# Two output tiles of a feed-forward chunk multiplied side by side, matmuls alternating between PSUM banks

## What is computed

```
def swiglu(x, w_gate, w_up, w_down):
    return (jax.nn.silu(x @ w_gate) * (x @ w_up)) @ w_down

f = swiglu(rms_norm_2(h, ffn1_norm_pre[l]), ffn1_w_gate[l], ffn1_w_up[l], ffn1_w_down[l])
h = h + 0.5 * rms_norm_2(f, ffn1_norm_post[l])
```

## Time and profile before

| what | value |
|---|---|
| median of 3 runs | 2175.87 us (2174.8 to 2176.27) |
| span of the profiled execution | 2173.0 us (its own time is not listed) |
| instructions | 24012 |
| PE busy | 92% |
| DVE, ACT busy | 53%, 37% |
| mean granted TensorE clock | 0.956 of full speed |
| transfers | 91 GB/s on average |

### The profile page before, as it was taken

How to read it: one execution, slowest core, us unless ns; L and a number is a source line. 1 busy time by engine, 2 the same in 40 slices (tenths; PEclk the granted TensorE clock), 3 DMA queues, 4 the chain that set the end, 5 groups by cost and what they waited for, 6 DMA issues and landing times.

```text
span 2173.0 us, 24012 instructions
## 1 busy us (share of the span) xinstructions
PE 2001.3 (92%) x8722; PEld 1578.5 (73%) x8722; DVE 1157.6 (53%) x1447; ACT 793.2 (37%) x971; POOL 43.3 (2%) x103
## 2 busy tenths in 40 slices
PE   4899999989999999799999997899996989999997
PEld 3687888866777777477888885676664757888885
DVE  4545666469354454455433456489744555433455
ACT  2326554233355544333222233223435243222232
POOL 2000000000000000000000000000000000000000
PEclk7899999989999999899999998999998989999997
DMA  8234556411222121023324322232211223324321
GB/s 309 91 113 140 182 160 178 145 58 59 77 59 59 39 59 39 20 78 97 92 87 111 97 73 82 77 98 78 57 41 39 78 58 97 92 87 111 97 73 63
DMA packets 293433, 198.28 MB, mean 91 GB/s; under 512 B 6690, under 2 KB 283508, under 8 KB 293364
## 3 DMA queue, kind: packets, MB, share of 16 engines
q1 hardware_dynamic: 284148, 163.79, 26.1%
q0 software_dynamic: 9216, 33.56, 4.6%
HBM read 195.21 MB, written 2.11 MB: 91 GB/s over the span
## 4 chain that ended last, share of the span: by engine, by line
PE 81%; DVE 10%; ACT 4%; issue 3%; SPq 1%; DMA 1%; DVEq 0%; ACTq 0%
PE acc L567 20%; PE acc L569 20%; PE acc L568 20%; PE acc L734 3%; PE acc L736 3%; PE acc L735 3%; PE ob L792 2%; PE sc L751 2%; DVE s_rstd L1416 1%; ACT s_w_high L1000 1%; PE acc L942 1%; PE ob L775 1%; DVE s_k_rt L1607 1%; PE acc L944 1%; PE acc L943 1%
## 5 line engine op out<-in xcount | busy, mean ns | idle before, releaser
L567 PE MATMUL acc<-s_h_high,s_w_high 128*128 128x512 f32 x1376 | 551.5, 401 | 38.2 <-DVE s_h_low L1389 16.9
L568 PE MATMUL acc<-s_h_low,s_w_high 128*128 128x512 f32 x1376 | 541.0, 393 | 0.0
L569 PE MATMUL acc<-s_h_high,s_w_low 128*128 128x512 f32 x1376 | 540.8, 393 | 0.0
L1378 DVE TENSOR_TENSOR s_w_low<-s_raw,s_w_high 128x2048 fp32r<-128x2048 f32 x160 | 366.7, 2292 | 301.9 <-ACT s_w_high L1000 301.4
L567 PEld LDWEIGHTS acc<-s_h_high,s_w_high 128*128 128x128 f32 x1376 | 261.5, 190 | 105.8 <-issue 41.6
L1000 ACT ACTIVATE s_w_high<-s_raw 128x2048 fp32r<-128x2048 f32 x160 | 305.0, 1906 | 9.9 <-DVE s_cols L1471 9.8
L569 PEld LDWEIGHTS acc<-s_h_high,s_w_low 128*128 128x128 f32 x1376 | 261.6, 190 | 55.4
L568 PEld LDWEIGHTS acc<-s_h_low,s_w_high 128*128 128x128 f32 x1376 | 262.1, 190 | 54.2 <-issue 2.2
L567 PE MATMUL acc<-s_b_high,s_w_high 128*128 128x512 f32 x640 | 257.2, 402 | 34.3 <-DVE s_branch L1920 16.4
L568 PE MATMUL acc<-s_b_low,s_w_high 128*128 128x512 f32 x640 | 252.8, 395 | 0.0
L569 PE MATMUL acc<-s_b_high,s_w_low 128*128 128x512 f32 x640 | 252.5, 395 | 0.0
(11 more groups left out here) (242 smaller groups left out, 2129.9 us busy)
## 6 DMA issues: line engine op xcount, KB each, us to landing
s_raw<-in_a_w_in SPq DMA_DIRECT2D x48, 512.0 KB, 5.0
s_raw<-in_ffn_w_gate SPq DMA_DIRECT2D x44, 512.0 KB, 3.9
s_raw<-in_ffn_w_up SPq DMA_DIRECT2D x44, 512.0 KB, 5.1
s_raw<-in_w_in SPq DMA_DIRECT2D x36, 512.0 KB, 4.3
s_raw<-in_b_w_in SPq DMA_DIRECT2D x32, 512.0 KB, 5.0
s_ada_w<-in_a_ada_w POOLq DMA_DIRECT2D x24, 512.0 KB, 6.5
s_ada_w<-in_b_ada_w POOLq DMA_DIRECT2D x24, 512.0 KB, 4.4
s_raw<-in_ffn_w_down SPq DMA_DIRECT2D x32, 384.0 KB, 3.9
```

Source lines behind the costliest of these rows:

```text
L567: pe.matmul(acc[b][:, :], w_high[:, o:o + P], hi, start=(k == 0), stop=False, skip_group_check=grouped)
L568: pe.matmul(acc[b][:, :], w_high[:, o:o + P], lo, start=False, stop=False, skip_group_check=grouped)
L569: mm = pe.matmul(acc[b][:, :], w_low[:, o:o + P], hi, start=False, stop=(k == nk - 1), skip_group_check=grouped)
L1378: dve.tensor_tensor(w_low[:, w], raw[:, w], w_high[:, w].bitcast(F32), ALU.subtract).then_inc(w_ready, 1)
```

## The change

PE makes the gate and the up tile of a chunk together. For each slice of k it issues six matmuls, gate and up in turn: high x high for both, high x low for both, low x high for both. The tiles go to `acc[0]`, `acc[1]` for chunks of slot 0 and to `sc[0]`, `sc[1]` for those of slot 1. Before a chunk PE waits for both counts, in the loops for one chunk less than before. In layer 1 the matmul of the sum of squares now stands behind all 48 matmuls of the first chunk; in layer 2 each of the eight stands behind six matmuls. DVE reads from the new banks; its order and ACT's are as they were.

```
+        gu_bank = [[acc[0], acc[1]], [sc[0], sc[1]]]
...
+            def both(tq, s, ready=None, base=0, between=None):
+
+                for t in range(2):
+                    pe.wait_ge(evac[t], tq)
+                for k in range(KD):
+                    if ready is not None:
+                        pe.wait_ge(ready, base + k + 1)
+                    hi, lo = h_high[:, k * T:(k + 1) * T], h_low[:, k * T:(k + 1) * T]
+                    o = [s * SLOT + paired(k, t) for t in range(2)]
+                    for t in range(2):
+                        pe.matmul(gu_bank[s][t][:, :], w_high[:, o[t]:o[t] + P], hi, start=(k == 0), stop=False,
+                                  skip_group_check=True)
+                    for t in range(2):
+                        pe.matmul(gu_bank[s][t][:, :], w_high[:, o[t]:o[t] + P], lo, start=False, stop=False,
+                                  skip_group_check=True)
+                    for t in range(2):
+                        mm = pe.matmul(gu_bank[s][t][:, :], w_low[:, o[t]:o[t] + P], hi, start=False,
+                                       stop=(k == KD - 1), skip_group_check=True)
+                        if k == KD - 1:
+                            mm.then_inc(tile_ready, 1)
+                    if between is not None:
+                        between(k)
...
                     for s in range(2):
                         chunk(q0 + s)
-                        for t in range(2):
-                            first = part == "a" and s == t == 0
-                            if first and l == 2:
-                                pe.wait_ge(ms_ready, 6)
-
-                            product(t, t0 + s, s, paired, t, h_high, h_low, 0, KD,
-                                    *((h_ready, hb) if first else ()),
-                                    between=(lambda k: sum_square(6, k)) if first and l == 2 else None)
-                            if first and l == 1:
-                                sums(2)
+                        first = part == "a" and s == 0
+                        if first and l == 2:
+                            pe.wait_ge(ms_ready, 6)
+
+                        both(t0, s, *((h_ready, hb) if first else ()),
+                             between=(lambda k: sum_square(6, k)) if first and l == 2 else None)
+                        if first and l == 1:
+                            sums(2)
                     with pe.Fori(1, nk // 2) as i:
                         for s in range(2):
                             chunk(2 * i + (q0 + s))
-                            for t in range(2):
-                                product(t, 2 * i + (t0 + s), s, paired, t, h_high, h_low, 0, KD)
+                            both(2 * i + (t0 + s - 1), s)
...
-                            dve.tensor_tensor(sg[s][:, :], rstd[:, :], acc[0][:, :], ALU.mult).then_inc(evac[0], 1)
+                            dve.tensor_tensor(sg[s][:, :], rstd[:, :], gu_bank[s][0][:, :], ALU.mult).then_inc(evac[0], 1)
                             dve.wait_ge(tile_ready, 2 * n + (t0 + 2))
-                            dve.tensor_tensor(hd[s][:, :], rstd[:, :], acc[1][:, :], ALU.mult).then_inc(evac[1], 1)
+                            dve.tensor_tensor(hd[s][:, :], rstd[:, :], gu_bank[s][1][:, :], ALU.mult).then_inc(evac[1], 1)
```

## The result

The changed kernel takes 2185.04 us (median of 4 runs, 2182.53 to 2186.09) where the kernel before takes 2176.07 on the same chip (4 runs, 2174.8 to 2176.55): 9.0 us more, a ratio of 1.0041 with a 95% interval of 1.0027 to 1.0055. It is slower, by a little less than the 11.4 us of the forecast. The profile after is of the fastest of its four runs, 2182.53 us.

The account below looks back on a forecast made before the run. The prediction took TensorE's matmuls, at full clock spaced by their chain of weight loads, as the bound. Terms 1.5 + 0.9 + 3.4 + 3.6 + 2.0 = +11.4 us on 2175.87 gave 2187.3 us, range 2180 to 2192.

Parts of the forecast that it names:

- (a): Gate/up matmuls, 2112 in 44 chunks: alternating banks changes nothing, 0 us, as the chain of weight loads sets the spacing.
- (b): Second chunk of each layer: first-evacuation wait goes, but its weight split comes later; +1.5 us layer 1, +0.9 layer 2.
- (c): Behind the second chunk's wait in both layers: granted clock falls to half, 1.7 us lost each, +3.4 us.
- (d): Gate/up to down, four times: the down product waits for the last gate tile's evacuation, 0.9 us each, +3.6 us.
- (e): Down to gate/up part b, twice: first matmul waits for ACT's copy of the last down tile, 1.0 us each, +2.0.
- (f): Within the loops: nothing waits, as the needed evacuation is done a chunk earlier; no cost.
- banks pay: Rival, gate/up matmuls: surplus comes from accumulating in one bank and vanishes; -16.7 us, 2159.2 us, chance 6%.
- the split is hidden: Rival, second chunk of each layer: its weights are ready in time; +1.4 us, 2177.3 us, chance 7%.
- the clock cycles: Rival, gate/up matmuls: bank changes leave small idle times and the clock falls repeatedly; 42 us, 2229 us, chance 3%.

Follow-up runs that it names:

- e4: Kernel before, with gate/up matmuls using 64 of 128 weight columns, so shorter weight loads: 2175.92 us (one run).
- e5: Kernel before, with gate/up matmuls in the loops streaming 384 of 512 columns: 2084.74 us (one run).
- e2: Changed kernel, with the second chunk's weights split before the mean square in each layer's first chunk: 2180.88 us, ratio 1.0024 to the kernel before.
- e9: Changed kernel, with the second chunk's weight split moved behind the reciprocal: 2197.11 us, ratio 1.0102.
- e3: Changed kernel run again unaltered: 2185.67 us, ratio 1.0052 to the kernel before.
- e6: Changed kernel, with part b's chunks starting in the sc banks, its down products there too, and one evacuation less awaited: 2180.01 us, ratio 1.0024 to the kernel before.
- e7: Changed kernel with e6's border waits off and e2's earlier weight split together: 2175.37 us, ratio 1.0001 to the kernel before.
- e10: The kernel of e1 run once more: 2172.37 us against 2175.29 for the kernel before, ratio 0.9986.
- e1: Kernel before, with four gate/up banks but the two tiles still made one after the other: 2173.27 us against 2175.06, ratio 0.9993.

## Why the prediction was right, and where it was not

The direction, the time (2185.0 in 2180 to 2192) and the places were right. By its parts:

(a) *Alternating banks: 0.* Right, 434 matmuls in 98 us in both kernels. The reason given beside it was wrong: the surplus of 13.3 ns isn't the chain of weight loads. e4 shortened the loads without a gain, e5 showed the same 13.3 ns at another width. What carried the prediction was the other row, that a change of bank in the kernel before costs and saves nothing.

(b) *The wait before the second chunk: +1.5 and +0.9.* Right in place, cause and size (measured +1.4 and +0.9). The wait was to be 3.1 us and released by line 1378's split; it is 2.98. TensorE resumes 4.01 us after the sum starts, where 4.09 was worked out. e2 took that wait away and e9 lengthened it by moving nothing but the split. The cover for the third chunk's weights held by 0.85 us (their split ends at 995.05, the chunk starts at 995.90) where 0.8 was worked out, and e2 shows what happens without it.

(c) *Clock: +3.4.* This term was put too high. "I take the value of two of three" took for certain what happens in some executions. At the six waits of 2.98 us in the traces of the changed kernel, e3 and e6, the clock fell behind two, none of them in the changed kernel's own trace; the price of a fall, 1.7 us, was right. Two in six of 3.4 us is 1.1, and with that the sum would have been 9.1 us. That it meets the measured 9.0 so closely is luck: six waits are too few for the share, the second set of runs gave 10.6 us (2185.67 against 2175.06), and the traces of the changed kernel and of e3 are of executions 2.5 and 3.6 us below their medians, in which fewer falls than usual may lie. At 1.7 us a fall the term is between 0 and 3.4 us, and how large on average stays open.

(d) and (e) *Borders: +3.6 and +2.0.* Idle times of 0.60 where 0.8 was forecast, and 0.89 where 0.7; with the slower first steps behind them 0.76 to 0.88 us each against 0.9, and 1.13 to 1.17 against 1.0. e6 without them is 5.7 us under e3 by the medians and about 2.5 us in a layer by the traces, against the 5.6 of the sum.

(f) *Nothing in the loops.* Right, no idle time there: each stretch of the loops shows TensorE busy throughout.

Without (c) the sum gives 1.5 + 0.9 + 3.6 + 2.0 = 8.0 us; the two layers show 4.36 + 3.86 = 8.2.

Of the rivals, "banks pay" is refuted by the spacing, "the split is hidden" by the wait and by e2, "the clock cycles" by a clock of 1.00 through the loops and by e7. The Trainium skill's rule on oscillation with bank cycling (TensorE: Matmul & The Clock Gate, section "A second HAM failure mode: psum-queue depth-cycling") has no counterpart in any trace here: 434 matmuls in 98 us at clock 1.00 while every one changes bank.

What stays open is the time outside the layers. From trace to trace the stretches at half clock in the other stages move, and single runs of the kernel before lie anywhere from 2168.95 to 2179.02. Effects under 4 us had to be read from the layers in the traces or from many runs.

## What to carry to other kernels

Finishing two tiles together at the end of a chunk delays all that hung on the first one: look for what another engine, in its own program order, has queued behind that tile (here a weight split behind a statistic), and for counts that stand for "this bank is free" though another bank is meant. More banks with the old order gave 0.14% (e10; e1 alone was not clear), and the interleaving on top of them only cost; try the two halves of such a change apart. Before expecting anything of alternating banks, look at one existing change of bank in the trace: if the step across it is no shorter, nothing is to be had.

## What the runs showed of the hardware

Each of these matmuls at full clock takes its columns at 2.4 GHz plus 13.3 ns: 226.7 ns for 512 columns, 173.3 for 384. It was the same with one bank and with alternating banks, and a shorter weight load didn't lower it. At half clock the step is 0.427 us, 512 columns at 1.2 GHz with no visible surplus. The Trainium skill, TensorE: Matmul & The Clock Gate, section "Back-to-back issue gap", puts the surplus of an isolated matmul at 2.5 ns; these traces, in which a weight load stands before every matmul, show 13.3.

Weights of 64 columns made the matmul slower, not faster: 230 ns a step against 226.7, with loads of 0.14 us in place of 0.19. Why is open.

Behind idle times of 2.98 to 3.00 us the clock fell in some executions and not in others: in two of six before the second chunk, in eight of twelve before layer 1. Behind 7.16 us it fell both times; behind the 1.60 us at the second chunk, in the kernel before, it stayed at 1.00. The length of the last idle time doesn't decide alone. In an attention stage of the kernel before TensorE was little busy, and the clock was at half behind an idle time of only 1.45 us, which ends at 881.72 (columns as in rows 3):

```profile
878.00:881.70 3.70, 1.06 (x4) 0.28 (x2) 0.42 (x2) 3.67 (x8) 0.00 (x0) 0.95 0.00 0
881.70:890.00 8.30, 3.59 (x5) 1.69 (x6) 4.63 (x8) 2.88 (x4) 0.00 (x0) 0.50 0.01 2
```
